# RWKV-7 rounds of a hybrid layer: products with a unit matrix in place of transposes, level and filler products issued in turn, and one wide product for two sets of rows

## What is computed

```
def step(S, inp):
    rt, wt, kt, vt, kkt, at = inp
    sa = einsum('rbhvk,rbhk->rbhv', S, -kkt)
    S = S * wt[..., None, :] + sa[..., None] * (kkt * at)[..., None, :] + vt[..., None] * kt[..., None, :]
    return S, einsum('rbhvk,rbhk->rbhv', S, rt)
```

## Time and profile before

| | |
|---|---|
| median of 3 runs | 2029.03 us (2028.51 to 2032.57) |
| the profiled execution's own time | 2030.1 us |
| its span | 2028.3 us |
| granted TensorE clock, mean | 0.96 |
| TensorE busy | 1836.2 us, 91% |
| VectorE, ScalarE, GpSimd busy | 961.1, 606.9, 780.0 us |

### The profile page before, as it was taken

One profiled execution on the slowest core, in us unless ns is written; L12 is line 12 of the kernel. 1 busy time (PEld: TensorE's weight loads), 2 busy tenths in 40 slices (PEclk: granted clock), 3 DMA queues, 4 the chain that ended last, 5 costly groups with the idle time before them and its releaser, 6 DMA issues. The chain is left out here.

```text
span 2028.3 us, 49121 instructions
## 1 busy us (share of the span) xinstructions
PE 1836.2 (91%) x20798; PEld 1727.9 (85%) x20798; DVE 961.1 (47%) x1619; ACT 606.9 (30%) x1339; POOL 780.0 (38%) x622
## 2 busy tenths in 40 slices
PE   6499799998899678888876999999999999999998
PEld 3488799787899577777755999999999999999998
DVE  7701854578433545555537455242424242424264
ACT  4412244333113555655533232020101010101034
POOL 3502242343762323235535313434343434344460
PEclk8699899899999799999997999999999999999999
DMA  9555110102111000000013101111111111111112
GB/s 310 176 186 195 29 38 21 30 1 97 41 40 29 6 7 6 4 4 5 5 37 109 38 22 36 48 37 47 36 47 36 47 38 49 37 52 31 52 53 94
DMA packets 148182, 110.33 MB, mean 54 GB/s; under 512 B 13298, under 2 KB 144393, under 8 KB 147757
## 3 DMA queue, kind: packets, MB, share of 16 engines
q1 hardware_dynamic: 148013, 107.83, 17.4%
HBM read 93.17 MB, written 14.55 MB: 53 GB/s over the span
## 5 line engine op out<-in xcount | busy, mean ns | idle before, releaser
L253 PE MATMUL banks<-Z_r 128*128 128x384 f32 x2016 | 350.8, 334 | 0.0
L253 PEld LDWEIGHTS banks<-Z_r 128*128 128x128 f32 x2016 | 349.5, 188 | 0.2
L2733 DVE SCALAR_TENSOR_TENSOR XT<-banks,MOD,XT 128x128 f32 x224 | 110.8, 516 | 226.0 <-PE banks L253 225.2
L3067 ACT ACTIVATE PAD<-banks 128x384 f32<-128x384 f32 x96 | 47.2, 492 | 503.0 <-PE banks L2962 502.7
L235 POOL TENSOR_TENSOR Z_r<-Z,ones 128x512 fp32r<-128x512 f32 x56 | 77.1, 1376 | 254.4 <-DMA Z<-in_mlp_w 254.4
L235 POOL TENSOR_TENSOR W_r<-Z,ones 128x1024 fp32r<-128x1024 f32 x32 | 77.1, 2409 | 240.7 <-DMA Z<-in_mlp_w 240.7
L3183 DVE TENSOR_TENSOR PAD<-PAD 128x384 f32<-128x384 f32 x96 | 99.1, 1032 | 142.7 <-ACT PAD L3067 142.6
L2962 PE MATMUL banks<-HT_r,W_r 128*128 128x384 f32 x768 | 149.1, 335 | 2.5 <-ACT HT_r L3034 1.6
L2962 PE MATMUL banks<-YT_r,W_r 128*128 128x384 f32 x768 | 148.6, 334 | 0.0
L2962 PE MATMUL banks<-HT_r,Z_r 128*128 128x384 f32 x768 | 148.5, 334 | 0.0
L2962 PEld LDWEIGHTS banks<-HT_r,W_r 128*128 128x128 f32 x768 | 134.4, 188 | 3.4 <-issue 1.9
(11 more groups left out here) (415 smaller groups left out, 3952.5 us busy)
## 6 DMA issues: line engine op xcount, KB each, us to landing
Z<-in_w_mod SPq DMA_DIRECT2D x16, 1024.0 KB, 5.2
Z<-in_mlp_w SPq DMA_DIRECT2D x32, 512.0 KB, 4.2
Z<-in_mlp_w SPq DMA_DIRECT2D x58, 256.0 KB, 2.7
YT<-in_w_in SPq DMA_DIRECT2D x18, 512.0 KB, 3.9
XT<-in_w_mod SPq DMA_DIRECT2D x8, 1024.0 KB, 10.8
residual<-Z SPq DMA_DIRECT2D x1, 4608.0 KB, 17.5
low_part<-XT_r SPq DMA_DIRECT2D x1, 4608.0 KB, 15.4
XT<-low_part SPq DMA_DIRECT2D x8, 576.0 KB, 5.5
```

The costliest lines, as they stand in the source:

```text
L253: mm = nc.tensor.matmul(self.bank(slot, g), w[slot][:, k, :], x(k, g), start=(n == 0 and k == 0), stop=(n == 2 and k == self.blocks - 1))
L2733: ins = nc.vector.scalar_tensor_tensor(out=x, in0=S.PS[3 * slot + g][:, a:b], scalar=S.MOD[:, ds(col, 1), c:c + 1].rearrange("p a b -> p ( ...
L3067: nc.scalar.activation(R[slot][:, grp(g)], up.bank(slot, g), ACT.Relu).then_inc(up.drained[g].sem, 1)
```

## The change

- The odd fillers are no longer transposes: each is 12 diagonal products of 64 x 64 rows with a unit matrix (`near(1, left, unit, "turned")`), and ScalarE copies the bank with one instruction of 128 x 384 in place of four of 64 x 192.
- A level product and its filler are issued in turn, in place of one after the other. A filler of 6 wide products goes with two level products to each.
- The third filler of a level comes after both `tz_pe`, no longer between them.
- B's rows times A's rows and times R's rows become one product of 128 columns, in the head (`gram_run`, banks 0 and 1 for d = 0, banks 4 and 5 for d = 1). Fillers 4 and 6 are empty. The part for d = 0 goes in turn with `q_run`; the part for d = 1 stands behind it and ahead of `u_pe`. Its two masked results are `LP` and `RB`, and `RB` is doubled.
- TensorE now waits for R's rows (`r_rows`) at the start of the step; `turns` go to banks 2 and 3.

```diff
-        self.AKRK, self.RB = HA.cut(2, 2, NP, 2, N), both(HA)
+        self.AKRK, rb = HA.cut(2, 2, NP, 2, N), both(HA)
+        self.RB = [[rb[:, d, :, :, :] for d in range(2)], [x.cut(2, NP, N) for x in (PD[2], rs)]]
...
+    def gram_banks(d):
+        x = S.PSALL[:, 4 * d:4 * d + 2, 0:2 * HW]
+        return x.rearrange("p c (q x n) -> p c q x n", q=NP, x=2)
+
+    def gram_run(d, par):
+        run = [one(gram_banks(d)[rows_of(h), c, p, :, :], C.BT[par][rows_of(h), d, p, cols(c)],
+                   C.ARR[par][rows_of(h), d, :, p, cols(c)]) for c in range(2) for p in range(NP) for h in range(2)]
+        run[-1] = (run[-1][0], "gram_l")
+        return run
... (filler)
-            done(pe, "copied" if b else "masked", n, m)
+            done(pe, "copied" if b else "masked", n, m if b else min(m, 2) + (m == 5))
...
-            for p in range(NP):
-                src = {"B": C.BT[par][:, d, p, :], "K": C.KT[:, d, p, :], "V": S.Z[:, 6 + p, tok:tok + P]}[x]
-                run.append(((lambda p=p, src=src: nc.tensor.transpose(S.PS[1][:, p * P:(p + 1) * P], src, S.ident[:, :])), None))
-        elif m in (2, 3):
-            run = near(0, tokens(C.BT[par], m - 2), tokens(C.RR[par], m - 2), "gram")
-        else:
+            left = {"B": tokens(C.BT[par], d), "K": tokens(C.KT, d),
+                    "V": lambda c, p, y, h: S.Z[y, 6 + p, tok + N * c:tok + N * c + N]}[x]
+            run = near(1, left, unit, "turned")
+        elif m in (0, 1, 4, 5):
... (round_pe)
-            done(pe, "masked", r, 6)
+            done(pe, "masked", r, 4)
+            done(pe, "rb", r, 2)
...
-                grams += near(d, tokens(C.BT[1 - par], d), tokens(C.AR[1 - par], d), "gram_l")
-        alternate(q_run(r, par, 0) if r is not None else [], grams)
+            done(pe, "r_rows", n, 2)
+            grams = [gram_run(d, 1 - par) for d in range(2)]
+        alternate(q_run(r, par, 0) if r is not None else [], grams[0])
+        if r is not None:
+            done(pe, "grown", r, 10)
+        alternate(grams[1])
...
-                    alternate(lt_run(d, i))
-                    alternate(beside)
+                    far = lt_run(d, i)
+                    if len(beside) == len(far):
+                        alternate(far, beside)
+                    else:
+                        alternate(far[0::2], far[1::2], beside)
                 for d in range(2):
                     tz_pe(pe, n, d, i)
-                    if d == 0:
-                        beside = filler(pe, n, 1 - par, 3 * i - 1, a)
-                        alternate(beside)
+                alternate(filler(pe, n, 1 - par, 3 * i - 1, a))
... (turned_act)
-        for c in range(2):
-            for h in range(2):
-                src = S.PS[1][rows_of(c), 0:NP * P].rearrange("p (q h n) -> p q h n", h=2, n=N)[:, :, h, :]
-                ins = nc.scalar.copy(x[rows_of(h), d, c, :, :], src)
+        nc.scalar.copy(x[:, d, :, :, :].rearrange("p c q n -> p (c q n)"), bank(1)).then_inc(f["copied"].sem, 1)
... (round_dve, after the masks of L)
+            for d in range(2):
+                nc.vector.tensor_tensor(C.RB[1 - par][d], gram_banks(d)[:, :, :, 1, :], by_chunk_mask(d, LEVELS + 1),
+                                        ALU.mult).then_inc(f["rb"].sem, 1)
... (the two masks of RB in the level section go; two of the other four are renumbered)
```

More of the change, by code:

```diff
@@ L1934, in recur_c @@
                      k_rows=2, r_rows=2, gram_l=2, masked_l=2, unit_l=2, seeded=4, l_turned=2, first=2,
-                     lt=10, zm=10, tz=10, grown=10, gram=6, masked=6, turned=6, copied=6,
+                     lt=10, zm=10, tz=10, grown=10, rb=2, gram=4, masked=4, turned=6, copied=6,
                      q=2, q_copied=2, u=2, u_copied=2, state=2, y=2, added=2, new_state=2, y_added=2)
@@ L2108, in filler @@
             tok = direction_tiles(pe, n)[0][d]
-            for p in range(NP):
-                src = {"B": C.BT[par][:, d, p, :], "K": C.KT[:, d, p, :], "V": S.Z[:, 6 + p, tok:tok + P]}[x]
-                if x == "K" and p == 0:
-                    done(pe, "k_rows", n, d + 1)
-                run.append(((lambda p=p, src=src: nc.tensor.transpose(S.PS[1][:, p * P:(p + 1) * P], src, S.ident[:, :])), None))
-            run[-1] = (run[-1][0], "turned")
-        elif m in (2, 3):
-            run = near(0, tokens(C.BT[par], m - 2), tokens(C.RR[par], m - 2), "gram")
-        else:
+            if x == "K":
+                done(pe, "k_rows", n, d + 1)
+            left = {"B": tokens(C.BT[par], d), "K": tokens(C.KT, d),
+                    "V": lambda c, p, y, h: S.Z[y, 6 + p, tok + N * c:tok + N * c + N]}[x]
+            run = near(1, left, unit, "turned")
+        elif m in (0, 1, 4, 5):
             d, c = m // 4, m % 2
@@ L2138, in round_pe @@
             done(pe, "b_rows", n, 2)
-        grams = []
+        grams = [[], []]
         if n is not None:
-            for d in range(2):
-                grams += near(d, tokens(C.BT[1 - par], d), tokens(C.AR[1 - par], d), "gram_l")
-        alternate(q_run(r, par, 0) if r is not None else [], grams)
+            done(pe, "r_rows", n, 2)
[4 more added lines that the diff above has]
+        alternate(grams[1])
         if r is not None:
@@ L2152, in round_pe @@
             for d in range(2):
-                turns += near(d, lambda c, p, x, h, d=d: C.LP[x, d, c, p, :], unit, "l_turned")
+                turns += near(2 + d, lambda c, p, x, h, d=d: C.LP[x, d, c, p, :], unit, "l_turned")
         alternate(q_run(r, par, 1) if r is not None else [], turns)
@@ L2334, in state_dve, with by_chunk_mask @@
         ins.then_inc(f["y_added"].sem, 1)
+    def by_chunk_mask(d, i):
+        return C.mask[:, d, i, :].unsqueeze(1).unsqueeze(1).to_broadcast([P, 2, NP, N])
     def masked_dve(dve, n, k):
         done(dve, "gram", n, k + 1)
[L2338 to L2346, removed]
+        d, c = k // 2, k % 2
+        two = C.mask[:, d, LEVELS:LEVELS + 2, :].unsqueeze(1).to_broadcast([P, NP, 2, N])
+        nc.vector.tensor_tensor(C.AKRK[:, d, c, :, :, :], bank(0).rearrange("p (q x n) -> p q x n", x=2, n=N), two,
+                                ALU.mult).then_inc(f["masked"].sem, 1)
     def zm_dve(dve, n, i, d):
@@ L2360, in first @@
                 done(dve, "l_turned", n, d + 1)
-                nc.vector.tensor_tensor(C.TW[:, d, 0, :, :, :].rearrange("p c q n -> p (c q) n"), by_block(bank(d)),
+                nc.vector.tensor_tensor(C.TW[:, d, 0, :, :, :].rearrange("p c q n -> p (c q) n"), by_block(bank(2 + d)),
                                         mask(d, 0, 2 * NP), ALU.mult).then_inc(f["first"].sem, 1)
@@ L2366, in round_dve @@
                 done(dve, "gram_l", n, d + 1)
-                nc.vector.tensor_tensor(C.LP[:, d, :, :, :].rearrange("p c q n -> p (c q) n"), by_block(bank(d)),
-                                        mask(d, LEVELS, 2 * NP), ALU.mult).then_inc(f["masked_l"].sem, 1)
+                nc.vector.tensor_tensor(C.LP[:, d, :, :, :], gram_banks(d)[:, :, :, 0, :], by_chunk_mask(d, LEVELS),
+                                        ALU.mult).then_inc(f["masked_l"].sem, 1)
+            for d in range(2):
+                nc.vector.tensor_tensor(C.RB[1 - par][d], gram_banks(d)[:, :, :, 1, :], by_chunk_mask(d, LEVELS + 1),
+                                        ALU.mult).then_inc(f["rb"].sem, 1)
         if r is not None:
```

9 lines of the change are left out of this document (3 added, 6 removed).

## The result

The changed kernel takes 2047.58 us (median, 2035.59 to 2049.23, 5 runs) against 2028.51 us before, ratio 1.0078 (95% interval 1.0047 to 1.011). With more runs later it took 2044.57 us against 2026.01 us, ratio 1.0090 (1.0072 to 1.0108). By the ratios it is slower by 16 to 18 us where 21 us faster were forecast. The ratios leave out one execution of 4952.61 us, of a kernel further down, whose cause was not looked for.

The account below looks back on a forecast made before the run. TensorE's queue was taken as the bound. Gain 4.0 less head 0.95 and supply 0.5 gave 2.55 us for eight steps, 20.4 us, plus 0.9 us in the first: 21.3 us, median 2007.7 us; range 1996 to 2020 us.

Parts of the forecast that it names:

- What bounds it now: Whole step: TensorE busy 91% of the span; level section, 19.21 of 21.45 us busy, taken as TensorE's own queue.
- the text's own signs of being wrong: Paired runs near 1.3 us, level section above 19 us, "issue" above 3 us a step, or waiting for R's rows.
- Instruction supply: Each step: 78 more matmul instructions cost 0.5 us, between nothing and one more longest stall of 0.6 us.
- Turned fillers, 2.3 us gain: Level section: four turned fillers beside level products, overlapped, take 0.75 in place of 1.32 us, gaining 2.3 us a step.
- Rule of the transposes: Turned fillers: if transposes were four times faster than unit-matrix products, total near 2063 us; chance one in a hundred.
- Head, loss 0.95 us: Step's head: wide products hold q to their pace, so u starts at 3.15 in place of 2.20 us.
- the lower bound of the text: Head: if q were not held, u would wait for the grams until 2.56 us, loss 0.35 us.
- What is late next: Level section: remaining waits on other engines, such as 0.8 us at (3,1) and 0.75 us before the next step.
- the walk: Level section: four levels timed from the rows' durations at 4.3, 3.9, 4.55 and 4.7 us.
- Level section 17.45 us: Level section of a step: 17.45 in place of 21.45 us, a gain of 4.0 us.
- First step, gain 0.9 us: First step, without a chain: level section gains 3.5 us, grams alone at low clock cost 2.6 us, gain 0.9 us.
- The slower one: Level section and head: diagonal and crossed runs do not overlap, 2.0 us a step lost, 2047 us; chance 0.06.

Follow-up runs that it names:

- the two experiments: Kernel before plus 324 one-column products on idle quarters: ratio 1.0061; changed kernel with each turned filler as two 384-column products of zeros: 0.9953.
- the split run: Kernel with wide product, transposes, gram fillers in turn, third filler between both tz; wide product for d = 1 split around u: 2024.17 us, 0.9994 of kernel before.
- 1.0029: Changed kernel with the third filler between the two tz again: 2032.51 us, ratio 1.0029 to the kernel before.
- the run with few wide products: Changed kernel with each turned filler as two products of 384 columns of zeros in place of twelve of 64: 2019.17 us, ratio 0.9953.
- both pairs of runs here: Third filler between the two tz against after both: changed kernel, 1.0029 against 1.0090; with transposes and four-piece copies instead, 0.9984 against 1.0048.

## Why the prediction was wrong

- **What bounds it now.** The step that failed. "So the level section is TensorE's own queue" was read from 19.21 busy of 21.45 us and taken to mean array time, so that every product put on an idle quarter is free. TensorE's queue it is, but of instructions: a packet of 256 every 3.4 to 3.9 us. A whole step before has 1289 TensorE products by the profile's count and as many weight loads, 10.1 packets. At 3.74 us each, an estimate from the changed kernel's median, they need 37.7 us of its 39.3 us. So there was little to gain in a step without fewer instructions, and the change adds 6%. For the changed kernel the same reckoning, 1367 products, gives 10.7 packets and 39.9 us; the windows above sum to 40.17 us. Two of the text's own signs of being wrong came: a level section above 19 us (22.19), and "issue" above 3 us a step (5.1).
- **Instruction supply.** The prediction saw the term and mis-sized it: 0.5 us a step. Its own rows held the better figure. Eight packets in 32 us is 4.0 us a packet, and 156 more instructions a step are 0.61 of a packet: 2.3 us a step even at 3.74 us each, 20 us over nine tiles. The text counted 78 instructions and left out their weight loads, which take places too. By the two experiments it costs 9.5 to 12.9 ns an instruction, 1.5 to 2.0 us a step. Bounding it above by "one more stall like the longest" took the size of a stall for its price. A sign that could have warned is that these waits stand within runs of products, where no semaphore is waited for.
- **Turned fillers, 2.3 us gain.** The overlap itself came true: of filler 3 and its level product, 48 instructions start between 814.72 and 815.4 us, as the tz did in the earlier trace rows. It bought nothing: 48 array instructions beside as many weight loads take 96 places in the stream, by estimate 1.4 us at 14.6 ns, about the 1.32 us that level product and transposes took. Transposes are the cheaper form in that currency: three of them with their loads are 6 instructions, twelve products are 48.
- **Rule of the transposes.** The Trainium skill ("TensorE: Matmul & The Clock Gate", "Terms") has transpose mode four times faster for FP32. A turned filler of the changed kernel that no issue wait breaks lasts 0.87 us from its first start to its last end (from 706.35 us), against 0.55 us for the transposes, 1.6 times as much. In time on the engine that rule still does not fit; in instructions the transposes win by eight times, which the text did not weigh.
- **Head, loss 0.95 us.** Mis-sized, with the wrong wait. u starts 2.54 us after q (793.38 less 790.84), not 3.15 us, and the head costs 0.34 us. That this is near the lower bound of the text, 2.56 us, is luck: u waits there for the wide products, but in the trace it waits for ScalarE's copy of q, as before. q's first and last start lie 1.75 us apart in place of 1.40 us, so the wide products did slow q, by 0.35 us, and the copy and u come that much later. The 12 wide products for d = 1 fill the wait for the copy, which the earlier trace rows show as 0.57 us; the split run above bears this out.
- **What is late next.** The wait for ScalarE's copy at (3,1) came as forecast, 0.75 us for 0.8 us, in six of the eight steps, and the step's start waits 0.72 us for 0.75 us. But the walk set them against the kernel before, whose four-piece copy makes 0.58 us at the start anyway, and so booked the new place of the third filler at 0.15 us there. With the one-piece copy and the old place the wait at the start is gone. Against that stand the mask waits that the new place removes (7.2 us to 0.7 us in all). The ratios 1.0090 and 1.0029 put the net cost of the place at 12 us, the traces of the nine steps at 4 to 7 us.
- **Level section 17.45 us.** It took 22.19 us. The walk had each instruction's array time and each copy, and no stream.
- **First step, gain 0.9 us.** It lost 2.6 us. Its two windows, cut as in the earlier trace rows at the first level product and at the next step's start:

```profile
671.48:685.47 13.99, 10.79 (x253) 10.10 (x253) 6.03 (x10) 1.63 (x5) 7.97 (x8) 0.84 0.01 2
685.47:707.95 22.48, 16.68 (x730) 15.15 (x721) 11.56 (x20) 12.29 (x24) 3.35 (x8) 1.00 0.02 4
```

  The level section is 1.5 us longer, where a gain of 3.5 us was booked. The wide products cost close to what was booked (their starts spread over 4.73 us in place of 2.51 us), but the 96 products behind them then ran at a clock of 1.00 in place of 0.66 and gave 1.2 us back.
- **Rivals.** The slower one had the right sign and, by luck, the right time (2047 us), with the wrong mechanism: the diagonal and crossed runs do overlap. The Trainium skill ("TensorEngine Tiling (Array Packing)", gotcha 1) says that different row tiles cannot access the same PSUM bank at once, and the spacing that the text set against this does not decide it. Products of two heads in one bank start 0.01 us apart (814.89 and 814.90 us), but starts alone can't show that neither slows the other. On its quarter a product of 384 columns is followed by the next after 0.32 us in the run with few wide products, where products of 384 columns that use the whole array follow one another after 0.17 us in the kernel before. Two heads in one bank may well share its time, and a spacing of 0.06 us on a quarter fits that too. No run puts them in two banks, so it stays open. It concerns the kernels before and after alike. The mechanism that did decide stood in the text as a term, not as a rival.

## What to carry to other kernels

Count instructions as well as array time where a stretch is made of hundreds of small products: find the instruction packets in the trace, divide the instructions issued by them, and set packets times the spacing that they keep when the engine runs dry (a median of 3.74 us here) against the stretch. Where that is most of it, as in these steps (37.7 of 39.3 us), work moved onto idle quarters of the array gained nothing, and forms with fewer instructions did (two wide products in place of twelve). In both pairs of runs here that differ in it alone, a filler that another engine has to copy did better ahead of the product whose copy comes next in that engine's order than behind it (12 and 13 us).

## What was not expected of the hardware

- In the rounds, whose code is written out without loops, TensorE's instructions come in packets of 256 (16384 bytes), at the shortest 3.3 to 3.4 us apart in every kernel here. A packet takes 1.0 to 1.2 us to land in the median, and TensorE goes on 1.2 to 1.6 us after it landed when it had run dry.
- Such a stall has no name of its own in the profile: it is "issue". So is the wait for a copy at a step's start, so the packets have to be set beside it.
- Behind twenty bare semaphore increments on TensorE's queue the next product waited 2.16 us, 0.11 us for each. With these pauses the granted clock of a step was 0.80 in place of 1.00.
- 128-column products issued in turn with 64-column ones on other quarters slow them a little: 1.75 us in place of 1.40 us for the 24 of q, where half of these had a wide partner.
